# VectorE instead of GpSimd for 212 weight remainders, in a two-block transformer kernel in float32

## The reference, cut to what matters

```
first_block:   h = x + rmsnorm(mix(rmsnorm(x) @ w_in) @ w_out)            # attention + RWKV-7
               z = rmsnorm(h, ffn_norm_pre)
               f = (silu(z @ ffn_w_gate) * (z @ ffn_w_up)) @ ffn_w_down   # 1024 -> 2816 -> 1024
               h = h + rmsnorm(f, ffn_norm_post)
second_block:  proj = rmsnorm(h) @ w_in                                   # 12288 columns
               o_hg = HGRN2 (8 heads of 128, chunks of 64); o_ret = retention (4 heads, 256 / 512)
               x = h + (sigmoid(gate_a) * (o_hg @ w_branch_hg) + sigmoid(gate_b) * (o_ret @ w_branch_ret)) @ w_out
               x = x + peer_ffn(rmsnorm(x))       # queries, top 16 of 128 twice, 16384 experts as dense products
               return rmsnorm(x)
```

## Time and profile before

| | |
|---|---|
| median of 3 runs | 3546.33 us (3540.53 to 3547.3) |
| the profiled execution's own time | 3540.67 us |
| its span | 3538.9 us |
| mean granted PE clock | 0.976 of full speed |
| busy: PE / weight loads / DVE / ACT / POOL | 95% / 77% / 51% / 35% / 23% |
| chain that ended last | PE 83%, DVE 13%, ACT 2%, issue 1% |
| POOL, remainders at L1388 | 262 instructions, 650.8 us |
| DVE, remainders at L1868 | 206 instructions, 252.4 us |

### The profile page before, as it was taken

One profiled execution on the slowest core, in us unless ns is written; L12 is line 12 of the kernel. 1 busy time (PEld: TensorE's weight loads), 2 busy tenths in 40 slices (PEclk: granted clock), 3 DMA queues, 4 the chain that ended last, 5 costly groups with the idle time before them and its releaser, 6 DMA issues.

```text
span 3538.9 us, 50538 instructions
## 1 busy us (share of the span) xinstructions
PE 3372.6 (95%) x18594; PEld 2731.6 (77%) x18594; DVE 1788.7 (51%) x3417; ACT 1227.4 (35%) x1609; POOL 803.9 (23%) x334
## 2 busy tenths in 40 slices
PE   8998997999988999998999999999998999999998
PEld 6665875887667778877878888888887888888886
DVE  3565344331155523333134799988885344444443
ACT  2222223332355533333233443444443333333332
POOL 6440022444323233333444444200000000000000
PEclk9988999999999999999999999999999999999999
DMA  3110011332222222222323344455556665555542
GB/s 132 51 46 1 3 32 54 95 95 92 86 71 65 65 72 71 73 75 78 95 94 103 106 143 142 146 180 178 178 178 235 184 218 191 190 194 191 190 143 77
DMA packets 145944, 408.01 MB, mean 115 GB/s; under 512 B 11176, under 2 KB 43944, under 8 KB 143536
## 3 DMA queue, kind: packets, MB, share of 16 engines
q1 hardware_dynamic: 73472, 265.85, 24.6%
q10 hardware_dynamic: 72368, 140.68, 11.0%
HBM read 337.28 MB, written 69.21 MB: 115 GB/s over the span
## 4 chain that ended last, share of the span: by engine, by line
PE 83%; DVE 13%; ACT 2%; issue 1%; ACTq 1%; DMA 1%; DVEq 0%
PE bank L325 23%; PE bank L327 22%; PE bank L326 22%; PE bank L421 2%; PE bank L904 2%; PE bank L902 1%; PE bank L354 1%; DVE arena L1726 1%; PE bank L838 1%; ACT arena L945 1%; PE bank L478 1%; DVE arena L1855 1%; PE bank L333 1%; PE bank L440 1%; DVE arena L1818 1%
## 5 line engine op out<-in xcount | busy, mean ns | idle before, releaser
L325 PE MATMUL bank<-xs,ring_hi 128*128 128x512 f32 x2488 | 996.3, 400 | 52.7 <-DVE xs L1417 20.9
L327 PE MATMUL bank<-xs,ring_lo 128*128 128x512 f32 x2488 | 975.3, 392 | 0.0
L326 PE MATMUL bank<-xs,ring_hi 128*128 128x512 f32 x2488 | 974.9, 392 | 0.0
L1388 POOL TENSOR_TENSOR ring_lo<-ring,ring_hi 128x1024 fp32r<-128x1024 f32 x262 | 650.8, 2487 | 1061.4 <-ACT ring_hi L945 1061.4
L945 ACT ACTIVATE arena<-bank 128x512 f32<-128x512 f32 (+4 forms) x584 | 392.0, 705 | 1051.8 <-PE bank L327 750.0
L945 ACT ACTIVATE ring_hi<-ring 128x1024 fp32r<-128x1024 f32 x469 | 495.6, 1059 | 501.8 <-DMA ring<-weights 238.4
L325 PEld LDWEIGHTS bank<-xs,ring_hi 128*128 128x128 f32 x2488 | 470.8, 189 | 164.1 <-issue 25.8
L327 PEld LDWEIGHTS bank<-xs,ring_lo 128*128 128x128 f32 x2488 | 470.6, 189 | 101.7
L326 PEld LDWEIGHTS bank<-xs,ring_hi 128*128 128x128 f32 x2488 | 471.3, 189 | 98.5 <-issue 4.3
L1868 DVE TENSOR_TENSOR ring_lo<-ring,ring_hi 128x1024 fp32r<-128x1024 f32 x206 | 252.4, 1225 | 404.2 <-ACT ring_hi L945 404.1
L325 PE MATMUL bank<-gw,ring_hi 128*128 128x512 f32 x1024 | 398.5, 389 | 0.7 <-ACT arena L945 0.7
(11 more groups left out here) (269 smaller groups left out, 3742.5 us busy)
## 6 DMA issues: line engine op xcount, KB each, us to landing
ring<-weights SPq DMA_DIRECT2D x503, 512.0 KB, 3.6
hidden<-arena ACTq DMA_DIRECT2D x128, 256.0 KB, 4.0
gates<-arena ACTq DMA_DIRECT2D x16, 2048.0 KB, 6.6
arena<-hidden ACTq DMA_DIRECT2D x16, 2048.0 KB, 10.3
arena<-gates ACTq DMA_DIRECT2D x16, 2048.0 KB, 17.1
xres<-x_t ACTq DMA_DIRECT2D x4, 512.0 KB, 5.2
out_t<-arena SPq DMA_DIRECT2D x1, 2048.0 KB, 7.2
arena<-ret_decay ACTq DMA_DIRECT2D x1, 1024.0 KB, 5.8
```

Of the source, the lines that this page charges most:

```text
L325: pe.matmul(out_, wh, x[0], start=start, stop=False, skip_group_check=True)
L326: pe.matmul(out_, wh, x[1], start=False, stop=False, skip_group_check=True)
L327: return pe.matmul(out_, wl, x[0], start=False, stop=stop, skip_group_check=True)
L1388: pool.tensor_tensor(ring_lo[:, r, :], ring[:, r, :], ring_hi[:, r, :].bitcast(F32), ALU.subtract).then_inc(lo_done, 1)
```

## The change

DVE makes the remainders of the 212 blocks from `B_FFN` to `B_U` - 1, by a function `dense` of its own, with a new semaphore `dense_lo`. POOL keeps the blocks before `B_FFN` and those from `B_U` to `B_S` + 1. The calls stand at chosen places of DVE's program: three after `norm_add` ahead of the feed-forward, two per pair of feed-forward blocks (one ahead of the wait for the pair, one behind its three steps), 24 in a row after that, one in each HGRN2 head between L1710 and L1712 and three behind the state chain, twelve per retention head, five per merge step ahead of its products, one per step of the output projection, and one per query block behind the eviction as far as `B_U`. PE's wait in `ready` follows.

```diff
-                if n < B_S:
+                if n < B_FFN:
                     pe.wait_ge(w_split, it * per + (n + 1))
+                elif n < B_U:
+                    pe.wait_ge(dense_lo, it * per + (n - B_FFN + 1))
+                elif n < B_S:
+                    pe.wait_ge(w_split, it * per + (n - B_U + B_FFN + 1))
@@ POOL
-            first = -(-B_FFN // RING)
-            for n in range(B_FFN, first * RING):
+            first = -(-B_U // RING)
+            for n in range(B_U, first * RING):
                 remainder(n % RING, n, w_split)
@@ DVE
+            def dense(n, it=0, per=0):
+                r = n % RING
+                ve.wait_ge(dense_hi, it * per + (n - B_FFN + 1))
+                TTN(ring_lo[:, r, :], ring[:, r, :], ring_hi[:, r, :].bitcast(F32), ALU.subtract).then_inc(dense_lo, 1)
+
+            for b in range(3):
+                dense(B_FFN + b)
             norm_scale(2, "ffn_pre", 2, 0)
@@ feed-forward pair
+                    dense(B_FFN + 2 * j + 3, i, 4)
                     ve.wait_ge(evac, i * 4 + q + 2 * j + 2)
...
                     TTN(lo, gu[:, 4 + j, :], hi.bitcast(F32), ALU.subtract).then_inc(ffn_pair, 1)
+                    dense(B_FFN + 2 * j + 4, i, 4)
                 st.leave()
             q += 2 * KF
+            for b in range(3 * KD):
+                dense(B_DOWN + b + 3)
@@ HGRN2 head
                 TTN(ch(tile(H_["CC"])), cu, cu[:, :, MID:MID + 1].to_broadcast([P, NCH, C]), ALU.subtract).then_inc(hg_dve, 1)
+                dense(B_HG + 3, h, 4)
                 ve.wait_ge(hg_act, h * 6 + 2)
...
+                for b in range(4, 7):
+                    dense(B_HG + b, h, 4)
                 ve.wait_ge(hg_act, h * 6 + 6)
@@ retention head
+                    dense(B_RET + 2 * k + 3, h, 12)
                     ve.wait_ge(evac, h * 12 + q + 2 * k + 2)
...
                     ve.wait_ge(rt_dve, h * 12 + 2 * k + 3)
+                    dense(B_RET + 2 * k + 4, h, 12)
+                for b in range(7, 10):
+                    dense(B_RET + b, h, 12)
...
+                for b in range(10, 15):
+                    dense(B_RET + b, h, 12)
                 ve.wait_ge(rt_act, h * 9 + 9)
@@ merge
-                if k == KD - 1:
-                    for m in range(KD - 1):
-                        xs_lo(4, lambda m: tile(MRG + m), m)
+                for b in range(3, 8):
+                    if k == KD - 1 and b == 5:
+                        for m in range(KD - 1):
+                            xs_lo(4, lambda m: tile(MRG + m), m)
+                    dense(B_MERGE + 5 * k + b)
                 ve.wait_ge(evac, q + 4)
@@ output projection, behind L1793
+                dense(B_WOUT2 + k + 3)
@@ queries, behind L1798
+                if B_PQ + k + 3 < B_U:
+                    dense(B_PQ + k + 3)
```

More of the change, by code:

```diff
@@ L211, in build @@
         w_split = sem("weights_split")
-        split_hi, dense_hi = sem("split_hi"), sem("dense_hi")
+        split_hi, dense_hi, dense_lo = sem("split_hi"), sem("dense_hi"), sem("dense_split")
         first_hi = sem("first_block_hi")
```

## The result

The changed kernel takes **3519.38 us** (median of 4 runs, 3516.72 to 3522.66), the kernel before, run beside it, 3545.19 us (4 runs, 3540.53 to 3547.3): a ratio of 0.9929 with a 95% interval from 0.9912 to 0.9947. That is 25.8 us faster, where 25.9 were predicted.

What follows compares the result with a forecast made beforehand. PE, busy 95%, was taken to lose time only in pauses where POOL holds DVE off. Waits of 17.7 us plus clock losses of 8.2 made 25.9 us, from 3546.33 to 3520.4 us; range 3511 to 3538.

Steps and rivals of the forecast that it cites:

- What bounds the kernel: Whole kernel: PE is busy 95% of the span, so moving 212 instructions counts only through PE's pauses.
- DVE is held off by POOL: Norms and HGRN2 heads: long DVE instructions, 1.41 to 2.80 us, are held off by POOL and end where its instruction ends.
- Norms: Ahead of the feed-forward: two adds finish 4.03 us earlier, 0.82 us of three remainders stick out, net gain 3.2 us.
- End of gate and up: PE waits for L1681, which falls from 2.59 us beside POOL to 0.69: gain 1.9 us.
- HGRN2 waits: Eight HGRN2 heads: PE's waits at L779 for the state chain's last step go, gain 11.7 us.
- PE waits only 1.46 for them: HGRN2 head: two long L1726 give back 2.82 us, but PE's wait for them is only 1.46, so no more is gained.
- The cover on DVE: HGRN2 heads: DVE's pauses hide the added remainders at no cost; if this failed, up to 1.23 us per head, 9.8 in all.
- The clock in HGRN2: Heads 5 and 8: two drops of PE's clock, 2.85 us each, are avoided: gain 5.7 us.
- The clock after gate and up: From 827.5 to 833 us: the clock loss behind PE's pause is avoided, gain 2.5 us.
- rival A: PE's clock: the waits go, but the clock losses stay or move to other heads; 3528.6 us, chance 0.26.
- I take all three as avoided: Behind gate and up and in HGRN2 heads 5 and 8: all three clock drops go, 2.5 + 5.7 = 8.2 us.
- Merge start: The first remainder, made by DVE behind its 24 splits, is ready at 1618.8 us, PE having started at 1619.85: gain 1.0 us.

Runs made afterwards that it cites:

- experiment 2: Changed kernel, but DVE makes only the 32 HGRN2 remainders and POOL the other 180, as in the kernel before: 3523.88 us, ratio 0.9933 to the kernel before.
- experiment 1: Changed kernel with HGRN2's 32 remainders back on POOL, DVE making the other 180: 3546.96 us, ratio 0.9991 to the kernel before.
- experiment 4: Changed kernel with the first three feed-forward remainders back on POOL, a single run: 3527.35 us.
- experiment 3: Changed kernel, with POOL also running 30 needless subtractions of constants in HGRN2: 3529.87 us, ratio 0.9939 to the kernel before.
- experiment 5: Changed kernel with two DVE remainders per HGRN2 head moved ahead of the state chain, plus one needless product: 3536.15 us, ratio 0.9962 to the kernel before.
- experiment 6: Changed kernel with the merge start's first two remainders behind the 8th and 16th of DVE's 24 splits, ACT rounding earlier: 3508.68 us, ratio 0.9881 to the kernel before.
- experiment 7: Changed kernel with the last remainder of the last merge step moved behind the merge products, a single run: 3521.22 us.
- experiment 8: Changed kernel with two merge-start remainders moved among the 24 splits and the last merge step's remainder behind its products: 3506.79 us, ratio 0.9885 to the kernel before.

## Why the prediction was right, point by point

**What bounds the kernel.** Right: of 212 moved instructions only those count beside which DVE's work was what PE waited for. Experiment 2 shows it in numbers: 32 of them bring 20.1 us. "What stands there is DVE" left out the longest line of the same list, PE behind ACT at L354; the norms' 3.5 us were won there.

**DVE is held off by POOL.** Right, shown both ways: POOL's work back, its length back (experiments 1 and 4); POOL reading for nothing, and DVE long again (3); POOL idle, and no step of DVE's long (after, 5). The two-input and scaling instructions with all operands in SBUF were the long ones. They end not exactly "where a POOL instruction ends" but a little behind it: 0.08 us for both L1726 of rows 6, 0.55 us for both adds of rows 4, which take 0.74 alone. The chain's other step, which reads one operand from PSUM, took 292 ns on average in the kernel before (L1724, 294 at most) and 292 after (L1741). The Trainium skill (SBUF — State Buffer, Who interferes with whom) says that VectorE and GpSimd have one pair of SBUF ports in common, that whoever takes it blocks the other for a whole instruction, and that a VectorE instruction with at most one SBUF input outside the two-port modes isn't touched. The traces agree with both halves: 1.61 us at L1755 of experiment 3 beside a POOL instruction of about 1.9, and 0.29 at L1724.

**Norms, 3.2 predicted, 3.55 measured.** The step was right and the remainder that "sticks out" a little too large. Timeline of DVE, after:

```profile
558.51 0.75 DVE L1431 SCALAR_TENSOR_TENSOR arena<-arena,par 128x512 f32<-128x512 f32 x1
559.29 0.75 DVE L1435 SCALAR_TENSOR_TENSOR arena<-arena,par 128x512 f32<-128x512 f32 x1
...
567.55 1.29 DVE L1436 TENSOR_TENSOR xres<-xres,arena 128x512 f32<-128x512 f32 x2
568.75 3.49 DVE L1676 TENSOR_TENSOR ring_lo<-ring,ring_hi 128x1024 fp32r<-128x1024 f32 x3
572.16 3.35 DVE L1425 RECIPROCAL arena<-arena 128x512 f32<-128x512 f32 x1
```

Neighbours on DVE overlap a little: from the end of the last add (567.55 + 1.29 = 568.84) to the start of the reciprocal it is 3.32 us, not 3 x 1.226 = 3.68. So 0.46 us stick out of the old pause of 2.86, and not 0.82: the adds' 4.01 less 0.46 are the 3.55.

**End of gate and up, 1.9 and 1.9.** Right: L1681's 2.59 became 0.69, and PE's pause 2.92.

```profile
824.09 0.69 DVE L1694 TENSOR_TENSOR hid<-gate_up,hid 128x512 f32 x1 [0.15 <-DVE hid L1693]
```

```profile
824.84 0.50 PE L329 MATMUL bank<-hid,ring_hi 128*128 128x512 f32 x1 [2.92 <-DVE hid L1694]
```

**HGRN2 waits, 11.7 predicted, 14.0 measured.** The mechanism was right, the term too small, in the step "PE waits only 1.46 for them". The recorded pause counts from a modelled end of the last matmul; the distance between starts is what is lost. Timeline of PE at L779 before, and at L783 after:

```profile
1014.69 0.39 PE L327 MATMUL bank<-xs,ring_lo 128*128 128x512 f32 x1
1016.53 0.49 PE L779 MATMUL bank<-arena 128*128 128x128 f32 x2 [1.46 <-DVE arena L1726]
```

```profile
1011.28 0.39 PE L331 MATMUL bank<-xs,ring_lo 128*128 128x512 f32 x1
1011.50 0.38 PE L783 MATMUL bank<-arena 128*128 128x128 f32 x2
...
1041.78 0.38 PE L783 MATMUL bank<-arena 128*128 128x128 f32 x2
```

1.84 us from start to start became 0.22: 1.62 less, and the first two products of L779 take 0.49 together against 0.38. The head is now 30.28 us (1041.78 - 1011.50) against 32.04, 1.75 less in each of eight. This could have been read before: 1.84 us from start to start, set against the 0.22 or so that two products without a pause are apart, is already 1.62.

The cover on DVE held, as assumed. DVE's timeline behind the chain of the first head, after:

```profile
1010.19 2.35 DVE L1676 TENSOR_TENSOR ring_lo<-ring,ring_hi 128x1024 fp32r<-128x1024 f32 x2
1013.28 1.22 DVE L1676 TENSOR_TENSOR ring_lo<-ring,ring_hi 128x1024 fp32r<-128x1024 f32 x1 [0.73 <-ACT ring_hi L949]
1016.73 3.35 DVE L1751 RECIPROCAL arena<-arena 128x512 f32<-128x512 f32 x1 [2.23 <-ACT arena L949]
```

The third waits 0.73 us for ACT's rounding, and 2.23 us of the pause ahead of the reciprocal are left.

**The clock in HGRN2, 5.7 and 5.7.** Right: over the whole stage the granted clock is 1.00 after, where it was 0.97, and 0.97 is what two stretches of 8 us at 0.57 leave of 263. Stretches of the kernel before and of the kernel after:

```profile
990.00:1253.00 263.00, 237.14 (x1198) 191.78 (x1199) 146.10 (x195) 135.17 (x170) 75.97 (x32) 0.97 0.20 64
```

```profile
986.00:1248.00 262.00, 247.85 (x1280) 203.74 (x1280) 157.61 (x239) 140.29 (x177) 0.00 (x0) 1.00 0.22 70
```

The Trainium skill (TensorE: Matmul & The Clock Gate, What's actually happening) has the clock set by how busy the engine has recently been. The runs agree that the drops hang on PE's pauses and on more than them: with pauses of 1.31 to 1.48 us ahead of the head's output products five of 24 heads lost it (two each in before and experiment 1, one in experiment 5), and in no two of the executions the same ones; with 0.65 or less in experiment 3, none of eight did, and with none (after, experiments 2, 4, 6, 7 and 8) none of 48. So the loss goes with this pause, though one execution of each kernel is behind each count.

**The clock after gate and up, 2.5 predicted, about 0.7 gained.** Here rival A was right in part. The pause became shorter but didn't go, and the clock still fell:

```profile
824.50:830.00 5.50, 5.16 (x16) 4.12 (x17) 1.42 (x2) 0.00 (x0) 0.00 (x0) 0.69 0.09 36
```

The failed step is "I take all three as avoided": two of them lost their pause, the third kept 2.9 of 4.8 us. From the first down product to the last it is 127.3 us in the kernel before and in experiment 2, which keeps the pause of 4.8, and 126.4 to 126.7 in the kernel after and the other seven experiments. That 0.7 and 1.66 us of the first head's wait are the 2.35 of the stretch up to the first L783.

**Merge start, 1.0 and 1.06; last merge step, -0.1 and 0.** Right. Timelines of DVE and PE at the start of the merge, after:

```profile
1579.86 14.54 DVE L1802 TENSOR_TENSOR o_lo<-arena,o_hi 128x512 fp32r<-128x512 f32 x24 [0.21 <-DVE arena L1795]
1594.32 3.48 DVE L1676 TENSOR_TENSOR ring_lo<-ring,ring_hi 128x1024 fp32r<-128x1024 f32 x3
```

```profile
1595.64 0.77 PE L329 MATMUL bank<-o_hi,ring_hi 128*128 128x512 f32 x1 [9.23 <-issue]
```

PE starts 15.78 us after the splits began, against 16.84 before. The prediction saw that the remainder waits behind the 24 splits but priced only what the change did there; a better order gives 10.7 us more, and the pause of 10.28 us that it removes stood in the same rows.

**Retention, down products, projection and queries, nothing.** Right to 0.2 us where the table has them alone: retention 309.4 and 309.4, queries and what follows 1664.3 and 1664.5.

That the sum came so close is in part luck, since errors cancel. By stretches it was 0.8 us short of 26.7: 2.3 too little for HGRN2's waits (14.0 less 11.7) and 0.3 for the norms, 1.8 too much for the clock behind gate and up. And the clock term of 5.7 rests on the two losses of one execution of the kernel before; with nearly the same pauses experiment 5 had only one.

## What to carry to other kernels

Look for VectorE instructions that take several times the median of their line and end where a GpSimd instruction ends, or up to their own length behind it. Where TensorE waits for such an instruction, move the GpSimd work that runs at that moment to VectorE, if it has a pause there; elsewhere the move is worth nothing. When such work comes to VectorE's queue, place each piece by what stands behind it: here two of them per head on the wrong side of a chain cost most of 16.8 us, and two moved from behind a long stream into the middle of it gave 10.7. For the price of a wait take the distance from start to start, not the recorded pause alone, and count a short pause that comes in every iteration as a risk for the clock too.

## What the runs showed of the hardware

- **The holding off goes both ways.** POOL's instruction took 6.06 us beside DVE's 24 splits, against a median of 2.40. The splits themselves took 14.54 us with POOL beside them and 14.54 without: at this one place the unbroken stream lost nothing.
- **The clock loss of a short pause comes and goes.** Eight equal heads with equal pauses lose it once or twice, at places that change between executions; each loss costs 2.85 to 2.9 us. Each head also has a pause of 0.98 us at L766 (L762 before) and one of 0.69 at L791 (L787 before) in every kernel here, and where these stand without the third no head lost the clock. Whether a head loses it with a third pause between 0.65 and 1.31 us is not shown. How much of a longer pause must go until the clock stays up isn't either: 2.9 us still lost some of it, and the merge start at 9.2 us lost as much as at 10.3 (0.50 for about 4.3 us in both).
- **An untouched stage sets the spread.** The start of the kernel up to the first norm took between 551.7 and 566.8 us in the profiled executions, in steps that no edit touches. From 100 to 350 us the clock was 0.83 in experiment 1 and 0.90 in experiment 2, at nearly equal busy time of PE:

```profile
100.00:350.00 250.00, 230.55 (x874) 146.72 (x872) 139.82 (x233) 54.58 (x129) 71.45 (x31) 0.83 0.11 32
```

```profile
100.00:350.00 250.00, 227.72 (x920) 142.69 (x918) 149.11 (x253) 59.18 (x141) 71.73 (x31) 0.90 0.10 32
```

  The 15.1 us between the shortest and the longest start are more than half of what this change brought. The sum from the first norm, which leaves it out, repeated to within 2 us in stretches that no edit touched.
- **Not tried:** a POOL instruction that only writes SBUF. The one of experiment 3 reads and writes, so whether writing alone holds DVE off is open.
